# Moving the sample attention of a hybrid layer into tile 0's U rows, in smaller units, with paired page-number loads

## The reference

```
# per token: projections of rmsnorm(x): u, cq, ckv, kr, qx, gates
# prompt:  MLA attention over its own 512 tokens; memory attention over 256 memory rows
# sample:  MLA attention of 4 tokens x 8 heads over 2048 past keys, which lie in 16 pages of 128 rows
lat_past = cache_kv_latent[l][page_table].reshape(8, 2048, 256)    # page: 128 x 256
kr_past  = cache_k_rope[l][page_table].reshape(8, 2048, 32)        # page: 128 x 32
s_past = (q_lat . lat_past + q_rope . kr_past) * scale ; s_new likewise, causal
p = softmax(concat(s_past, s_new)); o_lat = p_past @ lat_past + p_new @ c_kv ; o = o_lat @ w_uv
mem_o  = softmax(qx . mem_k * scale) @ mem_v                       # 256 memory rows, 4 heads of 128
# merge: g0*(pool_y @ w_pool_out) + g1*(mla_o @ w_mla_out) + g2*(mem_o @ w_x_out), then @ w_o
h = x + merged
# PEER: 128 experts of 16384 chosen per token by two top-16 searches
a = gelu(h_norm . peer_u[idx]) ; y = h + sum_k gate_k * a_k * peer_v[idx_k]
```

## Time and profile before

| what | us |
|---|---|
| median of three runs | 2352.08 |
| profiled execution | 2363.59 |
| its span | 2361.9 |
| first U0 gather | 686.61 |
| first V0 gather | 948.69 |
| first V1 gather | 1329.10 |
| busy: PE, DVE, POOL, ACT | 1303.4, 1167.5, 1099.9, 260.8 |
| moved by DMA | 687.44 MB |

### The profile page before, as it was taken

The page is one execution under the profiler, slowest core; times in us unless marked ns, Lnnn a source line. Parts: engine busy times, 40 slices in busy tenths (PEclk is TensorE's granted clock), DMA queues, the critical chain, the costliest instruction groups (busy, mean ns, idle before and its releaser), DMA issues.

```text
span 2361.9 us, 21631 instructions
## 1 busy us (share of the span) xinstructions
PE 1303.4 (55%) x6930; PEld 791.1 (33%) x6930; DVE 1167.5 (49%) x2824; ACT 260.8 (11%) x655; POOL 1099.9 (47%) x1226
## 2 busy tenths in 40 slices
PE   7997888999897657778820155400055400045513
PEld 5875545788785435434510011000011100001100
DVE  2104324511158876655298773188775088840060
ACT  2213223610120000011100000000000000000000
POOL 0004500000025434666566666666666666666664
PEclk9998897999999778889965577655577755567756
DMA  6214634055469889999999999999999999999997
GB/s 200 72 64 133 169 99 125 1 163 134 134 205 375 302 286 353 394 390 392 387 387 373 357 360 356 366 393 373 370 335 366 362 396 366 371 351 368 362 389 261
DMA packets 323510, 687.44 MB, mean 291 GB/s; under 512 B 37111, under 2 KB 174232, under 8 KB 323391
## 3 DMA queue, kind: packets, MB, share of 16 engines
q0 software_dynamic: 161792, 579.94, 65.3%
q1 hardware_dynamic: 161607, 106.13, 15.5%
HBM read 681.84 MB, written 4.18 MB: 290 GB/s over the span
## 4 chain that ended last, share of the span: by engine, by line
PE 28%; DVE 24%; POOL 11%; issue 11%; another core or an unknown queue 11%; DMA 7%; SPq 4%; DVEq 1%; ACT 1%; ACTq 0%
PE bank L671 21%; DVE arena L1872 20%; POOL arena L638 11%; DMA arena<-in_peer_v_dram,arena 5%; PE bank L1156 3%; PE bank L667 2%; DVEq L1808 1%; DMA arena<-in_w_pool_out_dram 1%; SPq L503 1%; SPq L507 1%; SPq L504 1%; PE bank L1013 1%; DMA arena<-in_peer_u_dram,arena 1%; PE bank L1131 0%
## 5 line engine op out<-in xcount | busy, mean ns | idle before, releaser
L638 POOL DMA_INDIRECT arena<-in_peer_u_dram,arena x544 | 510.7, 939 | 714.2 <-DVE arena L1856 382.5
L671 PE MATMUL bank<-arena 128*128 128x256 f32 (+7 forms) x2940 | 704.7, 397 | 102.7 <-DVE arena L1774 29.4
L1872 DVE CUSTOM_DVE_ANT_0 arena<-arena,bank 128x1024 f32<-128x1024 f32 x544 | 637.0, 1218 | 59.8 <-issue 55.4
L638 POOL DMA_INDIRECT arena<-in_peer_v_dram,arena x544 | 515.5, 948 | 295.3 <-issue 136.3
L671 PEld LDWEIGHTS bank<-arena 128*128 128x128 f32 (+2 forms) x2940 | 542.1, 193 | 264.2 <-issue 114.7
L1156 PE MATMUL bank<-arena 128*32 128x512 f32 x2176 | 384.5, 839 | 350.7 <-DMA arena<-in_peer_v_dram,arena 276.5
L667 PE MATMUL bank<-arena 128*128 128x128 f32 (+5 forms) x774 | 127.8, 313 | 560.5 <-issue 320.9
L667 PEld LDWEIGHTS bank<-arena 128*128 128x128 f32 (+5 forms) x774 | 106.1, 162 | 600.6 <-issue 362.0
L1156 PEld LDWEIGHTS bank<-arena 128*32 128x32 f32 x2176 | 84.6, 135 | 625.5 <-issue 621.6
L1901 DVE TENSOR_TENSOR arena<-arena,bank 128x1024 f32<-128x1024 f32 x5 | 6.1, 1221 | 377.0 <-PE bank L1156 222.9
L1192 ACT ACTIVATE arena<-bank 128x256 f32<-128x256 f32 (+12 forms) x325 | 126.4, 418 | 454.4 <-PE bank L671 192.4
(11 more groups left out here) (146 smaller groups left out, 751.9 us busy)
## 6 DMA issues: line engine op xcount, KB each, us to landing
arena<-in_w_in_dram SPq DMA_DIRECT2D x48, 512.0 KB
arena<-in_w_peer_q_dram SPq DMA_DIRECT2D x32, 512.0 KB
arena<-in_peer_u_dram,arena POOLq DMA_INDIRECT x544
arena<-in_peer_v_dram,arena POOLq DMA_INDIRECT x544
arena<-in_cache_kv_latent_dram POOLq DMA_DIRECT2D x64, 128.0 KB
arena<-in_cache_kv_latent_dram SPq DMA_DIRECT2D x64, 128.0 KB, 2.2
arena<-in_w_o_dram SPq DMA_DIRECT2D x8, 1024.0 KB, 11.0
arena<-in_w_in_dram SPq DMA_DIRECT2D x6, 1024.0 KB
```

What stands on the lines that cost most here:

```text
L638: pool.indirect_dma_start(out=ring[s % RING], out_offset=None, in_=table[0], in_offset=IndirectOffsetOnAxis(ap=ix, axis=0)).then_inc(land[ ...
L671: last = pe.matmul(dst, lhs(k), rhs(k), start=(k == 0), stop=(k == n - 1))
L1872: dve.tensor_tensor_reduce(ring[s % RING], ring[s % RING], h_dot, 1.0, 0.0, ALU.mult, ALU.add, act_a[:, p % 2, k:k + 1]).then_inc(u_free, 1)
```

## The change

Pages are taken two at a time (`PGRP = 2`, 16 steps). The whole sample attention, pages and memory, leaves its place before the prompt attention and becomes a background generator (`sample()` on PE, ACT and DVE) that runs ahead of `part(1)`: its 51 page units stand at U0's rows 3 to 98, its last three at 102 to 106, the 20 memory units from row 109 into V0. The 48 half merges move to V0's row 19 and on, the rest of part(1) into U1. It uses four PSUM banks: 4 and 5 for transposes, 6 for scores, 7 for probabilities and values, where it had all eight. All copies out of PSUM in it are ACT's. All pages are loaded by SP, after the query weights of part(0); two page numbers come by one register load. POOL loads none, and its clearing of `zw` moves from before gather 8 to before gather 124. Steps 1 and 2 of the loads wait for the query matmuls (`pq_mm`), step s >= 3 for the values of step s - 3; w_uv is loaded a second time. SBUF addresses move along with it (left out).

```diff
-PGRP = 4
+PGRP = 2
+HALVES = PAGES // PGRP
+STEPS = 2 * HALVES
-    u0, v0 = PLACE["u", 0, 0], PLACE["v", 0, 0]
-    ticks = [u0 + 2 + 5 * h // 2 for h in range(2 * MERGE)]
-    ticks += [v0 + 4 * r + 3 for r in range(12)]
-    ticks += [v0 + 52 + 2 * t for t in range(3)]
-    ticks += [v0 + 62 + 4 * t for t in range(3)]
-    ticks += [v0 + 76 + 4 * j for j in range(QJ + 2)]
+    u0, u1 = PLACE["u", 0, 0], PLACE["u", 1, 0]
+    ticks = [u0 + 3 + 23 * i // 12 for i in range(3 * (STEPS + 1))]
+    ticks += [u0 + 102 + 2 * i for i in range(3)]
+    ticks += [u0 + 109 + 7 * i // 4 for i in range(2 * (NB + 2))]
+    ticks += [u0 + 147 + 27 * h // 10 for h in range(2 * MERGE)]
+    ticks += [u1 + 22 + 27 * r // 10 for r in range(12)]
+    ticks += [u1 + 56 + 2 * t for t in range(3)]
+    ticks += [u1 + 64 + 3 * t for t in range(3)]
+    ticks += [u1 + 74 + 3 * j for j in range(QJ + 2)]
...
@@ SP, load_pages
-                if s == 2:
-                    sp.wait_ge(pool_mm, 2 * PG)
-                    sp.wait_ge(pool_d, PG)
                 if s >= 3:
                     sp.wait_ge(pv_mm, s - 2)
-                for j in range(2):
-                    for k in range(PGRP):
-                        n = (4 * a + j) * PAGES + g * PGRP + k
-                        page = sp.value_load(pagetab[0:1, n:n + 1], min_val=0, max_val=cache_lat.shape[1] - 1)
+                elif s >= 1:
+                    sp.wait_ge(pq_mm, QJ)
+                for j in range(4):
+                    n = (4 * a + j) * PAGES + g * PGRP
+                    _, pages = nc.values_load_multi_w_load_instructions(pagetab[0:1, n:n + PGRP], ...)
+                    for k, page in enumerate(pages):
...
@@ POOL: the loop that loaded pages for j = 2, 3 is gone
-                if s == 8:
+                if s == 124:
+                    pool.wait_ge(po_mm, 2)
                     pool.memset(zw[:], 0.0).then_inc(z_zero, 1)
...
@@ ACT
+            def sample():
+                act.wait_ge(id_next, 2)
+                for s in range(STEPS + 1):
+                    if s < STEPS:
+                        for u in range(5):
+                            act.wait_ge(pt_mm, 5 * s + u + 1)
+                            if s >= 1:
+                                act.wait_ge(ps_mm, s)
+                            ...                       # copy to latT or ropT
+                    yield
+                    ...                               # copy probabilities of step s - 1
+                    yield
+                    ...                               # exponentials of step s
+                    yield
...
@@ PE, ACT, DVE
-            bg = Background(part(1))
+            bg = Background(joined(sample(), part(1)))
```

More of the change, by code:

```diff
@@ L1 @@
 from contextlib import ExitStack
+from itertools import chain as joined
 import concourse.bass as bass
@@ L382, in hybrid_step @@
         mg_gate, mg_mm, mg_sig, mg_ev = sem("mg_gate"), sem("mg_mm"), sem("mg_sig"), sem("mg_ev")
-        ld_wo, wo0 = ld_smem, 64
+        ld_wo = [sem(f"ld_wo{i}") for i in range(3)]
         ld_hall, wo_mm, wo_ev = sem("ld_hall"), sem("wo_mm"), sem("wo_ev")
@@ new lines, in page_probs @@
+            def page_probs(s):
+                a, g = s // HALVES, s % HALVES
+                pe.wait_ge(ps_exp, s + 1)
+                if s >= 1:
+                    pe.wait_ge(pv_ev, s)
+                if s == HALVES:
+                    pe.wait_ge(po_ev, 1)
+                for k in range(PGRP):
+                    last = turn(bank[:, 7, k * P:(k + 1) * P], prob[:, s % 2, k * P:(k + 1) * P], P)
+                if g == HALVES - 1:
+                    last = turn(bank[0:NS, 6, 3 * P:4 * P], probn[:, a], P)
+                last.then_inc(pp_mm, 1)
@@ new lines, in page_values @@
+            def page_values(s):
+                i, a, g = s % 3, s // HALVES, s % HALVES
+                pe.wait_ge(pp_ev, s + 1)
+                for k in range(PGRP):
+                    for j in range(4):
+                        last = pe.matmul(bank[32 * j:32 * j + 32, 7, 256:512], probT[:, k, 32 * j:32 * j + 32],
+                                         lat[i][:, j, k], start=(k == 0), stop=(k == PGRP - 1 and g < HALVES - 1))
+                if g == HALVES - 1:
+                    for j in range(4):
+                        last = pe.matmul(bank[32 * j:32 * j + 32, 7, 256:512], newT[0:NS, 32 * j:32 * j + 32],
+                                         cnewt[0:NS], start=False, stop=True)
+                last.then_inc(pv_mm, 1)
@@ new lines, in mem_scores, with mem_out @@
+            def mem_scores(b):
+                pe.wait_ge(mt_ev, 2 * b + 2)
+                if b >= 1:
+                    pe.wait_ge(ms_exp, b)
+                for h in range(XH):
+                    last = pe.matmul(bank[32 * h:32 * h + TS, 6, 0:MEM],
+                                     qxs[:, h, b * TS:(b + 1) * TS], smT[:, h], start=True, stop=True)
+                last.then_inc(ms_mm, 1)
+            def mem_out(b):
+                pe.wait_ge(mo_ev, b + 1)
+                if b >= 1:
+                    pe.wait_ge(mx_ev, b)
+                turn(bank[:, 7, 384:512], smo[:, b % 2], P).then_inc(mx_mm, 1)
```

722 lines of the change are left out of this document (329 added, 393 removed).

## The result

The changed kernel takes 2409.95 us (median of four runs, 2406.32 to 2411.61) against 2352.15 in the same session: ratio 1.0236, 95% interval 1.0205 to 1.0266. It is slower by 2.4%, where 2% faster was forecast. Its profiled execution has a span of 2406.4 us against 2361.9.

What follows compares the result with a forecast made beforehand. PE's chain was taken to bound the part before the first gather, transfers the part after. Terms -156 + 14 + 93 and 0 for the rest gave -49 us, so 2303 against the median 2352.1, range 2245 to 2360.

Steps and rivals of the forecast that it cites:

- Bound: Whole execution: until the first gather at 686.6 us PE's order sets the time; after it, transfers count.
- Term 1: Before the gathers: sample attention leaves the stretch ahead of prompt attention, -156 us; first gather moves from 686.6 to about 531.
- Term 2: U0, first gather to last product: page steps beside the rows make it 290 us against 276, +14.
- the sum 14 + 15 x 14.5 + 11 + 47.5: U0: wait before step 1, 15 page steps, last step's landing, copies and scores, then rows 95 to 127: 290 us.
- The term's low end, 255: U0: with page steps at 11.3 us, loads are hidden and DVE's waits shrink, 255 us (-21).
- Rival 2: U0: page pieces take turns with row pieces, 20.8 us a step, U0 +108, total 2397; decides from 18; chance 0.14.
- Term 3: V0 and U1: full DMA engines also take merges, memory and w_uv, +93 us.
- the term's lower end: V0 and U1: the added 26.4 MB at the best rate seen, 392 GB/s, cost 67 us.
- The rest: V1 to the end, 1017 us at DMA share 0.96: same orders and waits, change 0.
- Rival 3: U1's end: V1's first weighing waits behind query units whose weights load at 10.4 us each; 40 us late, 2343; chance 0.12.
- waits and hand-overs: U0 before the change: some 45 of 276 us left after DVE's own work, among them waits for PE and ACT.
- The sum: Whole kernel: -156 + 14 + 93 = -49 us, giving 2303 for the median.

Runs made afterwards that it cites:

- comb3: Changed kernel with query units in V1, eight page numbers per load, at most six gathers queued in U0/U1, third memory buffer, split key/value semaphores; ratio 0.9927.
- no_wq: Changed kernel with ten of the 16 query weights of part(1) not loaded, units 6 to 15 reusing those of units 0 to 5; ratio 1.0264.
- depth6: Changed kernel with at most six gathers queued at the DMA in U0 and U1, all 12 buffers kept; ratio 1.0135.
- q_v1: Changed kernel with the 18 query units of part(1) at later ticks, six at U1's end and twelve between V1's weighings; ratio 1.0087.
- b_late: Kernel before with only the w_o, norm and query units of part(1) moved from V0 to the changed kernel's ticks in U1; ratio 1.0192.
- thin_u1: Changed kernel with at most four rows in flight from U1's row 40 on, 12 before; ratio 1.0269.
- no_pages: Changed kernel with pages loaded for the first three steps only, 104 of 128 left out, all computation kept; ratio 1.0121.
- pick_bg: Changed kernel with two page steps moved into each of picks 2 and 3, other steps 8 rows apart, memory units four rows later; ratio 1.0235.
- b_depth6: Kernel before with at most six gathers queued in U0 and U1; ratio 0.9953.

## Why the prediction was wrong, point by point

**Bound.** That the time has a part before the gathers, in which PE counts, held (term 1). That in the part after it only transfers count did not: at V1's start PE held the gathers back for 62.72 us.

**Term 1** was right: -152.8 against -156. The 48 matmuls of `prompt_kv` took 22.7 us, and 8 transposes 1.0 more, where 22.7 were worked out for both:

```profile
207.36 22.71 PE bank L663 x48
```

**Term 2** failed in size. From the first gather to the last product U0 took 336.9 us (533.8 to 870.7), not 290: 47 us too little in the term. The marks of the table, at gathers, show 34 of them (+48.3 against +14), because V0's first gathers go out before U0's last product, 26.5 us before it now and 14.0 before. The step that failed is the sum 14 + 15 x 14.5 + 11 + 47.5. The second step's loads started at 558.8, 25 us after the first gather and not 14 (+11). The 15 steps were issued until 798.3, 239.5 us and not 217.5 (+22). I had chosen 14.5 a step "because steps can be loaded under picks", and it was 16.0: 14.2 on average outside the picks, but 31.0 and 23.8 in picks 2 and 3, for three buffers are full well before a pick ends (each now holds two pages of a sequence and not four), and the chain cannot free one while DVE takes no maximum. The tail took 72.4 us and not 58.5 (+14); in it PE waits 8.64 and 4.54 us for memory rows, which have two buffers. The pair of pages saved less than thought: 3.10 us for two (565.06 to 568.16) instead of 2.83. The term's low end, 255, has no working; the sum at 11.3 a step gives 242. Rival 2's mechanism was not seen in its price: a step of 16.0 us, picks included, is under its 18.

**Term 3** was right in the number, +99 against +93, and partly by luck. The DMA time that V0 and U1 gained, share times duration, was 0.97 x 479.4 - 1.02 x 380.4 = 77 us and not 93.5; the rest is a hole in V0 while PE waits for memory rows. Without it, in comb3, the two take 459.0 us at a share of 1.02, +79. (The added bytes are 24 x 0.786 + 8.4 = 27.3 MB and not the 26.4 of the term's lower end, which makes that end 70 us instead of 67.)

**The rest** was forecast at 0, because it "has the same orders and waits", and became +50: V1's first 12 gathers took 79.0 us instead of 20.6 (+58), what follows them 8 us less. This is the step that failed most: the query units, moved to U1's end, put a new wait before V1's first weighing. Rival 3 named the place, the wait and the order of the engine (V1's first weighing behind the query units, 12 gathers to cover), but had a chance of 0.12 and a price of 40 us. Its reason was only half of it: no_wq shows that with weights at hand the stall is the same, and depth6 that without the slow matmuls the weights are next, at 11.0 us a unit where I had 10.4. I had read the cost of a query unit from V0 before, where rows wait for PE, and moved it to U1, where they don't. The trace of before already had the sign: 72 us of PE's weight loads idle for "issue" in U0 (`PEld bank L671 <- issue: 72.0, 19, 20.7`). I left it under "waits and hand-overs".

**The sum:** at the marks of the table two errors, 34 and 50 us, with term 3's 6 and term 1's 3, are the 93.5 us between -49 and +44.5. That the 50 come from the place of the query units and the depth of the queued gathers is shown (q_v1, b_late, depth6, thin_u1); by which way a deep queue slows PE is open. U0's part is only divided roughly, some 31 us of supply by no_pages and some 10 by pick_bg, which overlap.

## What to carry to other kernels

Before moving work between phases, ask in each who waits for whom: where the gathers wait for the engine, as in V1, no new ones are issued while it is behind; where another engine releases them, as DVE does in U1, they stay queued whatever it does (here for 70 us), so the duration measured in one phase is no price for the other. Keep the depth of what is queued apart from the number of buffers, and try it: one wait on a landed gather gave the kernel before 0.5%. And look at the buffers of a transfer that is moved beside dense rows. A sequence's memory rows landed in 4.0 and 5.4 us (keys and values, medians) in the kernel before, which had four buffers; in V0 PE waited up to 8.9 us for them with two, and 0.6 us with three and split semaphores.

## What the runs showed of the hardware

With up to 12 gathers of 512 KB queued and the DMA engines full (share 1.03), PE issued only some 45 matmuls of the query units in the 70 us from 1272 to 1342, many of them singly 2 to 3 us apart, with no wait that the profile shows; ACT stood too (40.5 us for "issue" in no_wq). With at most six queued, at a share of 1.04, it issued 22 matmuls in 4.86 us, and so it did with four at 0.99 (1281 to 1340 us of thin_u1). That the number of queued gathers makes it is shown by depth6 and thin_u1, and b_depth6 agrees. By which way is not shown. The profile has instruction packets of 16 KB in a queue of their own (q8), one in the 74 us from 1266 to 1340. The Trainium skill (Runtime: NRT & Kernel Launch, Instruction fetch mechanics) says that the sequencer fetches its next block by DMA while it executes the current one, and that this is mostly hidden. If that fetch stood behind the queued rows it could hold PE up. The trace speaks rather against it: between 1269.5 and 1357 us no packet of that queue is moved, only two of 8 KB in another (q14), while PE stalls and recovers. No run here separates it from other ways by which issuing could be held up.
